# Moving on-chip tiles to other addresses modulo 512 in a two-layer hybrid block

## The reference, cut to what matters

```
for l in range(DEPTH):
    x = x + 0.5 * swiglu_ffn(rms_norm(x, ffn1_norm[l]), ffn1_w_gu[l], ffn1_w_down[l])   # D_FF = 2816
    h = rms_norm(x, mix_norm[l])
    (x_r, g_r, q_b, c_kv, q_i, k_i, w_i, q_c, k_c, v_c, f_c, gate_a, gate_b, gate_c) = split(h @ w_in[l])
    o_a = rglru_branch(...)      # convolution, two small gates, a scan
    o_b = dsa_branch(...)        # top-64 of scores, attention over a latent
    o_c = fox_branch(...)        # causal attention with a forget bias
    merged = (sigmoid(gate_a) * (o_a @ w_branch[l, 0]) + sigmoid(gate_b) * (o_b @ w_branch[l, 1])
              + sigmoid(gate_c) * (o_c @ w_branch[l, 2]))
    x = x + merged @ w_out[l]
    x = x + memory_cross_attention(rms_norm(x, xattn_norm[l]), rms_norm(mem, mem_norm[l]), w_mq[l], w_mkv[l], w_mo[l])
    x = x + 0.5 * swiglu_ffn(rms_norm(x, ffn2_norm[l]), ffn2_w_gu[l], ffn2_w_down[l])
return rms_norm(x, final_norm)
```

## Time and profile before

| what | value |
|---|---|
| median of 3 runs | 1412.49 us |
| the profiled execution's own time | 1413.24 us |
| its span, first to last instruction | 1411.4 us |
| TensorE matmuls busy | 1372.3 us (97%), 8846 of them |
| TensorE weight loads busy | 1224.1 us (87%), beside the matmuls |
| VectorE busy | 944.3 us (67%) |
| ScalarE busy | 777.2 us (55%) |
| GpSimd busy | 131.2 us (9%) |
| mean rate of the DMA engines | 172 GB/s |
| granted TensorE clock, mean | 0.994 of full speed |

### The profile page before, as it was taken

The page is one execution under the profiler, slowest core; times in us unless marked ns, Lnnn a source line. Parts: engine busy times, 40 slices in busy tenths (PEclk is TensorE's granted clock), DMA queues, the critical chain, the costliest instruction groups (busy, mean ns, idle before and its releaser), DMA issues.

```text
span 1411.4 us, 23830 instructions
## 1 busy us (share of the span) xinstructions
PE 1372.3 (97%) x8846; PEld 1224.1 (87%) x8846; DVE 944.3 (67%) x1456; ACT 777.2 (55%) x1378; POOL 131.2 (9%) x219
## 2 busy tenths in 40 slices
PE   6999989999999999999999999999999999999998
PEld 5888879988999888888888888898989989888886
DVE  5666665868666567666676666658777666666665
ACT  5555555745654466454565555466546445655554
POOL 4010000022420100000010000000224001100000
PEclk9999999999999999999999999999999999999999
DMA  8677664544545545666666667446454554466662
GB/s 240 189 205 208 199 177 150 180 125 151 174 135 174 180 139 175 183 193 193 179 179 193 194 178 221 136 138 203 129 162 138 163 195 145 127 207 179 196 190 75
DMA packets 286384, 243.38 MB, mean 172 GB/s; under 512 B 14344, under 2 KB 263608, under 8 KB 286304
## 3 DMA queue, kind: packets, MB, share of 16 engines
q1 hardware_dynamic: 284176, 236.77, 55.5%
q10 hardware_dynamic: 1600, 4.25, 0.9%
q0 software_dynamic: 528, 1.26, 0.5%
HBM read 241.18 MB, written 1.27 MB: 172 GB/s over the span
## 4 chain that ended last, share of the span: by engine, by line
issue 64%; PE 26%; DVE 3%; ACT 2%; POOL 2%; POOLq 1%; DVEq 1%; DMA 1%; ACTq 0%
PE work L1548 16%; PE work L1623 2%; PE work L1570 2%; PE acc L1585 1%; PE work L1627 1%; PE acc L1775 1%; POOL diag L721 1%; ACT w_hi L507 1%; PE work L1763 1%; DVE w_lo L515 1%; POOLq L720 1%; DVE score L1350 1%; PE work L1754 1%; PE work L1698 0%; PE acc L1499 0%
## 5 line engine op out<-in xcount | busy, mean ns | idle before, releaser
L515 DVE TENSOR_TENSOR w_lo<-raw,w_hi 128x1024 fp32r<-128x1024 f32 x444 | 549.6, 1258 | 104.2 <-ACT w_hi L507 102.3
L507 ACT ACTIVATE w_hi<-raw 128x1024 fp32r<-128x1024 f32 (+1 forms) x442 | 450.5, 1053 | 25.6 <-PE acc L1585 25.6
L1623 PE MATMUL work<-act,w_hi 128*128 128x512 f32 x1408 | 439.2, 393 | 9.5 <-DVE w_lo L515 5.5
L1627 PEld LDWEIGHTS work<-act,w_lo 128*128 128x128 f32 x1408 | 265.0, 188 | 59.2
L1548 PE MATMUL work<-act,w_hi 128*128 128x256 f32 x1696 | 312.0, 282 | 4.2 <-DVE act L1131 2.1
L1627 PE MATMUL work<-act,w_lo 128*128 128x256 f32 x1408 | 278.8, 279 | 0.0
L1548 PEld LDWEIGHTS work<-act,w_hi 128*128 128x128 f32 x1696 | 262.2, 188 | 11.0 <-issue 6.2
L1548 PE MATMUL work<-act,w_lo 128*128 128x256 f32 x848 | 236.7, 279 | 0.0
L1623 PEld LDWEIGHTS work<-act,w_hi 128*128 128x128 f32 x1408 | 216.5, 188 | 13.4 <-issue 10.4
L821 ACT ACTIVATE gu_s<-work 128x256 f32<-128x256 f32 x176 | 58.1, 382 | 199.1 <-PE work L1627 199.1
L1548 PEld LDWEIGHTS work<-act,w_lo 128*128 128x128 f32 x848 | 159.1, 188 | 0.6 <-issue 0.5
(11 more groups left out here) (238 smaller groups left out, 1746.0 us busy)
## 6 DMA issues: line engine op xcount, KB each, us to landing
raw<-in_ffn_w_gu SPq DMA_DIRECT2D x174, 512.0 KB, 5.0
raw<-in_w_in SPq DMA_DIRECT2D x52, 1024.0 KB, 5.2
raw<-in_ffn_w_down SPq DMA_DIRECT2D x44, 1024.0 KB, 4.9
raw<-in_w_branch SPq DMA_DIRECT2D x12, 1024.0 KB, 5.0
raw<-in_w_mkv SPq DMA_DIRECT2D x8, 1024.0 KB, 5.2
raw<-in_w_out SPq DMA_DIRECT2D x8, 1024.0 KB, 4.9
raw<-in_w_mq SPq DMA_DIRECT2D x4, 1024.0 KB, 5.4
raw<-in_w_mo SPq DMA_DIRECT2D x4, 1024.0 KB, 4.8
```

Of the source, the lines that this page charges most:

```text
L507: eng.activation(halves(w_hi, slot, kind, part), halves(raw, slot, kind, part), ACT.Copy)\
L515: eng.tensor_tensor(halves(w_lo, slot, kind, part), halves(raw, slot, kind, part), halves(w_hi, slot, kind, part).bitcast(F32), ALU.subtra ...
L1623: pe.matmul(work[:, 2 * c + g, :], w_hi[:, slot, at_w:at_w + P], act[:, :, k, :], start=(k == 0), stop=False, skip_group_check=True)
L1627: mm = pe.matmul(work[:, 2 * c + g, 0:SEQ], w_lo[:, slot, at_w:at_w + P], act_hi[:, k, :], start=False, stop=(k == KT - 1), skip_group_che ...
```

## The change

No instruction is added, taken out or moved: the order on each engine is the same, and no wait is changed. Only places change. Six small tiles (`mx`, `nm`, `sm`, `ri`, `ms`, `rstd`, of 32 bytes each with the rounding) go from the end of the memory to places between large tiles, and `mem_x` with the two tiles over it (`fox_bias`, `mrg_lo`) goes from behind `x` to behind `pt`. The whole takes 229248 bytes as before.

```
--- before.py
+++ after.py
@@ -264,9 +264,7 @@
         x = at("x", [P, TT, D])
-        mem_x = at("mem_x", [P, TT, D])
-        fox_bias = at("fox_bias", [P, HEADS, SEQ], over="mem_x")
-        mrg_lo = at("mrg_lo", [P, KT, SEQ], F32R, over="mem_x")
+        mx = at("mx", [P, 4, 2])
         xr = at("xr", [P, BT, SEQ + CONV_W])
@@ -280,8 +278,11 @@
+        nm = at("nm", [P, 4, 2])
         act = at("act", [P, 2, KT, SEQ], F32R)
         act_hi, act_lo = act[:, 0, :, :], act[:, 1, :, :]
+        sm = at("sm", [P, 4, 2])
+        ri = at("ri", [P, 4, 2])
         o_hi0, o_lo0, o_hi1, o_lo1 = (at(name, [P, BT, SEQ], F32R) for name in ("o_hi0", "o_lo0", "o_hi1", "o_lo1"))
@@ -302,7 +303,12 @@
         lg = at("lg", [P, 2, 2, SEQ])
+        ms = at("ms", [P, TT])
+        rstd = at("rstd", [P, TT])
         pt = at("pt", [P, 2, 2, 2, P])
+        mem_x = at("mem_x", [P, TT, D])
+        fox_bias = at("fox_bias", [P, HEADS, SEQ], over="mem_x")
+        mrg_lo = at("mrg_lo", [P, KT, SEQ], F32R, over="mem_x")
@@ -337,8 +343,6 @@
-        ms = at("ms", [P, TT])
-        rstd = at("rstd", [P, TT])
@@ -346,10 +350,6 @@
-        mx = at("mx", [P, 4, 2])
-        nm = at("nm", [P, 4, 2])
-        sm = at("sm", [P, 4, 2])
-        ri = at("ri", [P, 4, 2])
```

## The result

The changed kernel takes 1418.49 us, the median of 6 runs (1415.84 to 1420.27), against 1411.95 us of the kernel before (6 runs, 1410.12 to 1412.88). The ratio is 1.0047, with a 95% interval of 1.0035 to 1.0058. The forecast was 1397.7 us and faster; the time is inside the stated range and on the other side of zero.

What follows compares the result with a forecast made beforehand. TensorE was taken as the bound, time being matmul count times pitch. Seven items summed to 14.8 us gained; 1413.24 less 14.8 is 1398.4, less 0.75 gives 1397.7 us, range 1374 to 1420 us.

Steps and rivals of the forecast that it cites:

- Nothing becomes late: With the pitch 2% better, VectorE would be at 68 to 69%, so nothing becomes late in place of TensorE.
- Items 3, 4 and 6: Gains: branches, 64 to 192, 2.5 us; `mem`, 0 to 32, 0.4 us; `mrg`, `last`, `o` on L1585, 1.8 us.
- item 6: `mrg`, `last` and `o` on L1585, 128 bytes further: 384 matmuls gain 4.7 ns each, 1.8 us.
- Item 1: `act` stationary-weight projections, L1548, distance 64 to 128: 2.2 ns a matmul, 5.6 us gained.
- item 2: Gate and up, L1623 and L1627, 64 to 128: 352 groups of eight gain 18.2 ns each, 6.4 us.
- Item 7: `h` on L1585, distance 192 to 128: 3 x 320 matmuls lose 2.35 ns each, 2.3 us lost.
- Item 5: `act` stationary on L1570 with 256 columns: 192 matmuls at 2.2 ns, 0.4 us gained.
- Rival C: 128 is a bad distance; `act` and `h` go to the worst levels: 14 us lost, 1427 us; chance 0.14.
- Rival A: Nothing moves: a unit's start in some cycle sets its level, new distances shuffle without trend: 1412.5 us; chance 0.18.

Runs made afterwards that it cites:

- shift_all: Kernel before with every tile, weights too, 64 bytes further up, all distances kept: 1412.44 us, ratio 1.0004.
- all_512: Kernel before with 512 bytes of small tiles between the weights and everything else: 1412.93 us beside 1411.24.
- the three kernels with one part each: Kernel before with only `act` at 128, only `h` at 128, or only the tiles that gained moved: ratios 1.0050, 1.0037, 0.9991.
- The map: Pitches by distance, from six kernels with `mem`, `act`, `o` and `h` at other distances, plus earlier traces; the six took 1405.03 to 1422.93 us.
- h_only: Kernel before with only `pt`, and `h` over it, moved from distance 192 to 128: 1417.00 us, ratio 1.0037.
- best: Kernel before with `act`, branches, `o`, `last`, `mrg_hi` at 192, `mem` 32, `h` 256, `mrg_lo` 0: 1403.21 us against 1411.54, ratio 0.9943.
- sw_b: Kernel before with distances `act` 256, branches and `o` 320, `mem` 96, `h` 320: 1422.36 us beside 1415.75.
- sw_d: Kernel before with distances `act` 160, branches and `o` 96, `mem` 32, `h` 160: 1422.93 us beside 1415.75.
- lo_512: Kernel before with 512 bytes of small tiles between `w_hi` and `w_lo`: 1412.91 us beside 1411.24.
- sw_g: Kernel before with distances `act` 384, branches and `o` 416, `mem` 352, `h` 32: 1421.90 us beside 1411.54.

## Why the prediction was wrong

**The bound was right.** The time moved with the pitch of TensorE's matmuls; VectorE, ScalarE and the sum of the waits stayed where they were (DVE 944.3 to 946.6 us, ACT 777.2 both times). "Nothing becomes late" held less well: VectorE's `merged` holds TensorE up for 1.2 us more.

**That distance is the lever was right.** shift_all, all_512 and the three kernels with one part each show it. Items 3, 4 and 6 of the sum came true in sign and roughly in size: branches 2.5 us forecast, 2.0 measured; `mem` 0.4 and 0.7; `mrg`, `last` and `o` 1.8 and 1.0. Only item 6 had a row at its new distance (`h` at 192 on L1585). For the branches at 192 and `mem` at 32 there was none on L1548, and that the straight line hit their sign is luck: on the same line 96 is as bad as 0.

**The step that failed is "I take the value between because 128 lies between the two distances that L1585 shows".** It assumed that pitch falls with distance in a straight line, from three distances on two different lines. The map shows no order at all. Item 1 forecast 5.6 us gained and it was 3.2 lost, item 2 forecast 6.4 gained and it was 3.6 lost: together 18.8 of the 20.7 us that lie between the forecast sum (-14.8) and the measured one (+5.9). Item 7, the one forecast as a loss, was 2.3 and became 2.8 us. Rows on one line would have warned: the slope of the 256-column matmuls came from L1548 at 0 and 64, that of the 512-column ones from L1585 at 64 and 192, and no line had shown three. The steps were coarse besides: the 4.7 ns on L1585 come from starts given to 0.1 us, and over the whole trace 233.4 less 229.5 is 3.9. Item 5, L1570 with `act`, forecast 0.4 us gained; its pitch rose from 116.5 to 118.7 ns, 0.4 us lost. And on L1585 the duration does not go with the level as the prediction says: `h` has 394 ns in the earlier trace rows, as `last` has, with 229.5 and 233.4 ns of pitch.

**The gate/up price was never in a row.** The slope of L1585, whose stationary operand is the activation, was put on L1623, where it is the weights. The map has the two lines go opposite ways: at 256 L1585 is at its best and gate/up at 1.394 us is among its worse ones.

**Rival C is what happened**, at about half its price: it had 14 us lost, and the median moved by 6.5. Projections lost 1.4 and not 2.2 ns, an eight of gate/up 11 and not 23 ns, `h` 2.9 and not 4.7 ns. Its point of decision, 1.39 us for an eight, was passed by little, 1.394. Its cause, a meeting of the two reads at 128, was not shown, and 128 is not the worst distance of any line. **Rival A** was wrong as a whole, since the pitches of the parts repeat from kernel to kernel, but the observation that fed it stands: units with the same distance can sit at 113.3 or 117.8 ns. In the changed kernel the branch units at 192 do so too: ten of the twelve have 113.3 ns and two 117.8. Distance sets how many units find the better level.

The rule that TensorE's two read ports are independent, from the Trainium skill ("TensorE: Matmul & The Clock Gate", part 2, and "SBUF — State Buffer", "Who interferes with whom"), would have given zero. h_only contradicts it: one large tile moved, the one line of the table that reads it changed, by 3.8 ns in 229.5, and the kernel took 4.9 us more. Whether it is the load that holds the stream was not shown.

That every operand begins a multiple of 512 bytes behind its tile, as said ahead of the prediction, is not so for the 96 matmuls of L1570 that move 144 columns: their weights begin 256 bytes further. They play no part, with 110.7 to 110.8 ns in every run here.

## What to carry to other kernels

In a kernel that TensorE bounds, addresses are worth about a percent: setting three residues gave 0.57% with not one instruction changed. But a pitch at a distance that was never run can't be interpolated from its neighbours. Map it, which is cheap: one profile gives the pitch of every line at once, and in this kernel eight steps of 32 bytes, counted as moving minus stationary, were enough. Map each line by itself, because the best distance of one is the worst of another. Add up the parts by their pitches, and expect some of the sum to come back as waits. Small tiles with no other place to be make good spacers.

## What was not expected of the hardware

- The pitch of a matmul with 128 stationary columns depends on the distance of the activation's and the weights' tiles: 113.7 (best) to 120.0 ns (sw_b) for 256 columns, 227.3 (best) to 234.2 ns (sw_d) for 512.
- It does not depend on the address itself (shift_all), and 512 bytes more change nothing (all_512, lo_512). In the map 256 bytes more change nothing either (128 and 384: 118.7 and 118.7 ns). 32 bytes make a difference (64 bytes 117.5, 96 bytes 119.9 ns).
- The direction matters: 192, which is -64 modulo 256, gives 114.8 ns and 64 gives 117.5. It goes by the roles, moving minus stationary: L1570 with `mem` at 96 has 117.4 ns and L1548 at 96 120.0 (sw_b), at 352 118.4 and 119.9 (sw_g).
- One distance can have two steady levels, 113.3 and 117.8 ns at 64 and at 192, and nearly every unit keeps the one it falls into; 3 of 54 projection units find the better one at 64 and 40 of 54 at 192. What picks it stays open, as does which two reads clash.
